# A fused fp32 transformer program on one core: stripes of eight columns in the second attention, output splits by pair, merged first tiles

## The reference, cut to what matters

```python
GRID_W, WIN_ROWS, WIN_COLS = 64, 8, 16          # 512 tokens are 8 rows of 64 columns
def neighborhood_attention(q, k, v, k_ctx, v_ctx, rpb):
    rows = n // GRID_W                           # 8
    kr = min(WIN_ROWS, rows)                     # 8: every query sees all rows
    col_start = jnp.clip(col - kc // 2, 0, GRID_W - kc)      # kc = 16
    col_mask = (col[None, :] >= col_start[:, None]) & (col[None, :] < col_start[:, None] + kc)
    def one_row(args):
        s_lat = einsum('bqhd,brkhd->bhqrk', qr, kb) * scale + bias
        s_lat = jnp.where(col_mask[...], s_lat, -jnp.inf).reshape(bsz, h, GRID_W, kr * GRID_W)
        s_ctx = einsum('bqhd,bchd->bhqc', qr, k_ctx) * scale
        p = softmax(concatenate([s_lat, s_ctx], axis=-1), axis=-1)
        o = einsum('bhqk,bkhd->bqhd', p[..., :kr * GRID_W], vb)
        return o + einsum('bhqc,bchd->bqhd', p[..., kr * GRID_W:], v_ctx)
```

## Time and profile before

| what | value |
|---|---|
| three runs, us | 2466.03, 2467.61, 2477.45; median 2467.61 |
| the profiled execution: its own time / span, us | 2472.82 / 2471.0 |
| granted TensorE clock, mean over the span | 0.989 |
| busy share | PE 96%, PE weight load 74%, DVE 48%, ACT 41%, POOL 15% |
| DMA | 77 GB/s mean, 190.64 MB |

### The profile page before, as it was taken

The page is one execution under the profiler, slowest core; times in us unless marked ns, Lnnn a source line. Parts: engine busy times, 40 slices in busy tenths (PEclk is TensorE's granted clock), DMA queues, the critical chain, the costliest instruction groups (busy, mean ns, idle before and its releaser), DMA issues.

```text
span 2471.0 us, 33313 instructions
## 1 busy us (share of the span) xinstructions
PE 2369.6 (96%) x12710; PEld 1816.9 (74%) x12710; DVE 1178.3 (48%) x1907; ACT 1010.6 (41%) x1667; POOL 376.7 (15%) x254
## 2 busy tenths in 40 slices
PE   7999999898999999989999999999999999999998
PEld 4888765466868776667776678888877667888886
DVE  5000554644442105664445556666454474666645
ACT  5111436544253425554325543333252474333422
POOL 2233001200332430003000210003400003000142
PEclk9999999999999999999999999999999999999999
DMA  7121331100231211113220122223322102322231
GB/s 309 51 69 60 116 118 48 52 1 1 65 114 60 77 60 69 53 39 105 77 85 18 35 94 94 93 94 96 100 86 86 60 1 73 98 94 94 94 101 43
DMA packets 51586, 190.64 MB, mean 77 GB/s; under 512 B 5723, under 2 KB 6107, under 8 KB 51196
## 3 DMA queue, kind: packets, MB, share of 16 engines
q1 hardware_dynamic: 51452, 188.78, 23.0%
HBM read 186.66 MB, written 2.10 MB: 76 GB/s over the span
## 4 chain that ended last, share of the span: by engine, by line
PE 89%; ACT 5%; DVE 4%; issue 2%; DMA 0%; POOL 0%; SPq 0%; DVEq 0%; ACTq 0%; POOLq 0%
PE PS L650 6%; PE PS L648 6%; PE PS L649 6%; PE PS L1772 5%; PE PS L1799 4%; PE PS L2404 3%; PE PS L2403 3%; PE PS L2405 3%; PE PS L1785 3%; PE PS L1479 3%; PE PS L602 3%; PE PS L603 3%; PE PS L601 3%; PE PS L810 2%; PE PS L808 2%; PE PS L809 2%
## 5 line engine op out<-in xcount | busy, mean ns | idle before, releaser
L648 PE MATMUL PS<-H_HI,W_SPLIT 128*128 128x512 f32 x672 | 265.5, 395 | 0.0
L650 PE MATMUL PS<-H_HI,W_SPLIT 128*128 128x512 f32 x672 | 264.9, 394 | 0.0
L649 PE MATMUL PS<-H_LO,W_SPLIT 128*128 128x512 f32 x672 | 264.5, 394 | 0.0
L497 POOL TENSOR_TENSOR W_SPLIT<-WT,W_SPLIT 128x1024 fp32r<-128x1024 f32 x43 | 104.5, 2429 | 615.9 <-ACT W_SPLIT L488 495.5
L465 ACT ACTIVATE W_SPLIT<-WT 128x1024 fp32r<-128x1024 f32 x80 | 84.8, 1060 | 267.3 <-PE PS L650 267.3
L1003 POOL TENSOR_TENSOR OUT_HALF<-WT,OUT_HALF 128x512 fp32r<-128x512 f32 x48 | 71.3, 1488 | 723.2 <-ACT OUT_HALF L967 723.2
L2758 DVE TENSOR_TENSOR W_SPLIT<-WT,W_SPLIT 128x1024 fp32r<-128x1024 f32 x80 | 98.0, 1225 | 150.1 <-ACT W_SPLIT L465 150.0
L2744 DVE TENSOR_TENSOR G_LO<-SB,G_HI 128x512 fp32r<-128x512 f32 x43 | 100.3, 2332 | 112.1 <-ACT G_HI L2565 112.1
L649 PEld LDWEIGHTS PS<-H_LO,W_SPLIT 128*128 128x128 f32 x672 | 126.0, 188 | 30.4 <-issue 0.5
L648 PEld LDWEIGHTS PS<-H_HI,W_SPLIT 128*128 128x128 f32 x672 | 126.2, 188 | 29.9 <-issue 0.5
L650 PEld LDWEIGHTS PS<-H_HI,W_SPLIT 128*128 128x128 f32 x672 | 126.2, 188 | 29.8
(11 more groups left out here) (354 smaller groups left out, 5494.6 us busy)
## 6 DMA issues: line engine op xcount, KB each, us to landing
WT<-weights SPq DMA_DIRECT2D x314, 512.0 KB, 3.5
SB<-weights SPq DMA_DIRECT2D x13, 512.0 KB, 13.4
SB<-rpb SPq DMA_DIRECT2D x8, 512.0 KB, 4.5
HT<-rpb SPq DMA_DIRECT2D x8, 512.0 KB, 4.4
XT<-tokens SPq DMA_DIRECT2D x4, 768.0 KB, 7.6
out<-HT SPq DMA_DIRECT2D x4, 512.0 KB, 3.2
SB<-late SPq DMA_DIRECT2D x1, 1280.0 KB, 5.8
SB<-con SPq DMA_DIRECT2D x1, 1248.0 KB
```

Source lines behind the costliest of these rows:

```text
L497: g.tensor_tensor(w[:, 1, :], W[:, slot, :], w[:, 0, :].bitcast(F32), ALU.subtract).then_inc(sem("w_lo"), 1)
L648: pe.matmul(PS[:, s, :], hi, H_HI[:, c, :], start=(c == 0), stop=False)
L649: pe.matmul(PS[:, s, :], hi, H_LO[:, c, :], start=False, stop=False)
L650: last = pe.matmul(PS[:, s, :], lo, H_HI[:, c, :], start=False, stop=(c == KC - 1))
```

## The change

1. **Neighbours.** att_od becomes an object of the subclass `Neighbours`. Image tokens are kept in stripes: token order is (stripe of 8 columns, row, column in the stripe), so that a stripe is 64 tokens. A step has 256 context keys and four stripes of image keys. Steps 1 to 3 take the queries of two neighbouring stripes; step 0 takes those of the two outer stripes (queries 0 to 63 and 448 to 511), whose keys are stripes 0, 1, 6, 7. The order is made where the window's norm is written (two `tensor_scalar` and two Ln with a rearranged view in place of one), and undone by the last product. Lag goes from 1 to 2, and DVE takes the first of two copy groups. The table of biases is 768 wide, not 1024.
2. **Outputs split by pair.** The splits of an output's input chunks move into the attention: ACT `split_hi` after unit u, DVE `split_lo` one step behind. PE's wait for the last product is gone; seven of tile 0's eight chunks (21 matmuls) are issued by `ahead_pe` right behind the last values and spread (in att_df ahead of the last unit's sums; in att_mla none). In att_mla the splits come in groups of 5, 2 and 1 chunks after units 3, 5 and 7.
3. **First tiles merged.** The tiles with the rotary key columns (`KROPE`) and with the gate's low rank columns (`GLR`) become one tile: 25 tiles in `ev_in`, 313 in all, every later tile one slot earlier in SP's order.
4. **The last two tiles of the last down projection** are split in the other order.

```diff
@@ Output
+            def ahead_pe(self, pe):
+                for c in range(KC - 1):
+                    self.chunk_pe(pe, 0, c)
             def pe(self, pe):
-                pe.wait_ge(sem("evac_dve"), ev_base[self.name][1])
...
@@ Output
+            def split_hi(self, act, c):
+                act.wait_ge(sem("at_out"), self.att.b["out"] + c + 1)
+                act.activation(self.O_HI[:, c, :], self.O[:, c, :], ACT.Copy).then_inc(sem("o_hi"), 1)
+            def split_lo(self, v, c):
+                v.wait_ge(sem("o_hi"), self.hi0 + c + 1)
+                v.tensor_tensor(self.O_LO[:, c, :], self.O[:, c, :], self.O_HI[:, c, :].bitcast(F32), ALU.subtract).then_inc(sem("o_lo"), 1)
@@ Pairs.act, Pairs.dve
+                    if s - self.lag - 3 in self.final:
+                        self.following.split_hi(act, self.final.index(s - self.lag - 3))
...
+                    if s - self.lag - 4 in self.final:
+                        self.following.split_lo(v, self.final.index(s - self.lag - 4))
@@ Window.split_hi
+                for k in {3: range(0, 5), 5: range(5, 7), 7: range(7, 8)}.get(u, ()):
...
+                    act.activation(self.O_HI[:, k, :], PROJ[:, ZA + self.order[k], :], ACT.Copy).then_inc(sem("o_hi"), 1)
@@ Pairs.masked
-                    if n > 512:
-                        v.tensor_tensor_reduce(out=self.SM[:, a, 512:n], in0=PS[:, self.bank(s, a) + 1, 0:n - 512],
...
+        class Neighbours(Pairs):
+            def key_parts(self, s):
+                t = self.steps[s][1]
+                if t == 0:
+                    return [(0, 0, 128), (128, 384, 512), (256, L, N)]
+                return [(0, L, N), (256, 128 * t - 128, 128 * t + 128)]
+            def queries(self, t):
+                return [(0, 0, 64), (64, L - 64, L)] if t == 0 else [(0, 128 * t - 64, 128 * t + 64)]
+            def place(self, ps, u, t):
+                return outer(ps) if t == 0 else ps[:, 128 * t - 64:128 * t + 64]
+            def last_product(self, v, dest, values, rows):
+                return v.tensor_tensor(stripes(dest), by_stripe(values), by_stripe(rows), ALU.mult)
@@ ev_in
-GLR, GK, GQ, GV, QLAT, KVLAT, KROPE, ZA, ZB = 0, 1, 3, 5, 9, 15, 17, 18, 22
-EV_CHUNKS = 26
+GLR, GK, GQ, GV, QLAT, KVLAT, ZA, ZB, ROW = 0, 1, 3, 5, 9, 15, 17, 21, 25
+EV_CHUNKS = 25
@@ feed-forward
+        def down_next(l, t):
+            return (FC - 1, FC - 2) if l == 1 and t == FC - 2 else () if l == 1 and t == FC - 1 else (t,)
```

More of the change, by code:

```diff
@@ L984, in dve @@
             def dve(self, v, add):
-                for c in range(KC):
-                    v.wait_ge(sem("o_hi"), self.hi0 + c + 1)
-                    v.tensor_tensor(self.O_LO[:, c, :], self.O[:, c, :], self.O_HI[:, c, :].bitcast(F32), ALU.subtract).then_inc(sem("o_lo"), 1)
+                self.split_lo(v, KC - 1)
                 h0 = split_at[self.following][0]
@@ L1387, in sums_ps, with split_hi, split_lo, ahead_pe @@
                 return PS[:, 6:8, :].rearrange("p b n -> p (b n)")[:, 0:N]
+            def split_hi(self, act, u):
+                for k in {3: range(0, 5), 5: range(5, 7), 7: range(7, 8)}.get(u, ()):
+                    if k >= 4:
+                        act.wait_ge(sem("at_out"), att_mla.b["out"] + 2 * (k - 4) + 2)
+                    elif k == 0:
+                        act.wait_ge(sem("at_out"), att_mla.b["out"] + 4)
+                    act.activation(self.O_HI[:, k, :], PROJ[:, ZA + self.order[k], :], ACT.Copy).then_inc(sem("o_hi"), 1)
+            def split_lo(self, v, u):
+                for k in {3: range(0, 5), 5: range(5, 7), 7: range(7, 8)}.get(u, ()):
+                    c = self.order[k]
+                    v.wait_ge(sem("o_hi"), k + 1)
+                    v.tensor_tensor(self.O_LO[:, c, :], PROJ[:, ZA + c, :], self.O_HI[:, k, :].bitcast(F32), ALU.subtract)\
+                     .then_inc(sem("o_lo"), 1)
+            def ahead_pe(self, pe):
+                pass
             def out_pe(self, pe):
@@ L1518, in out_act @@
             def out_act(self, act):
[L1519 to L1522, removed]
+                self.split_hi(act, 7)
                 for t in range(1, 8):
@@ L1600, in out_dve @@
             def out_dve(self, v):
[L1601 to L1604 removed]
+                self.split_lo(v, 7)
                 add = residual_one(v, "ev_out", N, lambda t, b: MOD[:, 16 + t, b:b + 1])
@@ L1714, in __init__ @@
                                 ("rows", 0 if gate else self.U), ("gated", self.U if gate else 0),
-                                ("half", 2 * self.S if mask and width > 512 else 0), ("out", self.U)]:
+                                ("out", self.U)]:
                     Pairs.total[name] += n
@@ L1798, in values @@
                     for a in range(2):
[L1799 to L1801 removed]
+                        x = self.PT[:, s % 2, (a * nb + c) * 128:(a * nb + c) * 128 + 128]
+                        last = pe.matmul(self.place(PS[64 * a:64 * a + 64, 6, :], u, t), self.v_of(pair, a, self.value_block(s, c)),
+                                         self.turned_block(t, x), start=(c == 0), stop=(c == nb - 1))
                 last.then_inc(sem("at_valued"), 1)
@@ L1807, in spread @@
                 for s in range(self.first[u], self.final[u] + 1):
-                    at = 128 * self.steps[s][1] - self.cols(u)[0]
+                    t = self.steps[s][1]
                     for a in range(2):
-                        last = pe.matmul(PS[64 * a:64 * a + 64, 7, at:at + 128], self.small(32, s, a).broadcast_to([128, 64]),
-                                         IDENT, start=True, stop=True)
+                        last = pe.matmul(self.place(PS[64 * a:64 * a + 64, 7, :], u, t), self.small(32, s, a).broadcast_to([128, 64]),
+                                         self.turned_block(t, IDENT), start=True, stop=True)
                 last.then_inc(sem("at_spread"), 1)
@@ L2291, in _ @@
             pe.wait_ge(sem("evac_act"), after("ev_in")[0] - 1)
-            pe.wait_ge(sem("evac_dve"), after("ev_in")[1] - 1)
+            pe.wait_ge(sem("evac_dve"), after("ev_in")[1])
             logits(0)
@@ L2373, in _ @@
             att_mla.pe(pe)
-            att_mla.wait(pe)
             pe.wait_ge(sem("gla_gated"), 1)
@@ L2380, in _ @@
             att_od.pe(pe)
-            att_od.wait(pe)
             out_od.pe(pe)
@@ L2414, in _ @@
             att_e.pe(pe)
-            att_e.wait(pe)
             out_e2.pe(pe)
@@ L2421, in _ @@
             att_df.pe(pe)
-            att_df.wait(pe)
             out_df.pe(pe)
```

201 lines of the change are left out of this document (115 added, 86 removed).

## The result

| | before | after |
|---|---|---|
| median of four runs, us | 2469.36 (2466.03 to 2477.45) | 2394.52 (2389.36 to 2395.21) |
| span of the profiled execution | 2471.0 | 2393.4 |
| PE, DVE, ACT busy, us | 2369.6, 1178.3, 1010.6 | 2309.7, 1147.9, 978.8 |
| mean granted clock | 0.989 | 0.988 |

A forecast was written before the change was run, and what follows sets the result against it. PE was taken as the bound, 89% of the chain that ended last. Terms of -59.7, -2.3, -3.9, -0.4, +1.8, -8.4, -1.9 and +0.5 sum to -74.3, from the median 2467.6 to 2393 us; range 2384 to 2406.

The forecast's parts named there:

- Second attention, -59.7: Steps go from 768 to 512 keys, 3.14 us each; a unit goes from 20.96 to 13.5 us, saving 59.7.
- Rivals A: Second attention: step 0's scores run only two tiles at a time, +6.9 us, 2400; chance 0.15.
- B: Second attention: PSUM writes in two runs cost double, about +8 to +10 us, 2402; chance 0.08.
- the bound with nothing taken off: Second attention: ACT at 12.3 and DVE at 13.3 us per unit with splits added and no work removed, under 13.5.
- Outputs: PE's waits before outputs shrink through early splits: out_od -2.3, out_e2 -2.4, ev_out -2.0 us.
- +3.2: att_mla: splits delay PE, some 2 us from the five on DVE and 1.2 from the group of two.
- att_df, +1.8: att_df and out_df: splits add 0.4 us to each of six units, +2.4; 0.7 of wait before the last sums saved.
- The part on att_e: att_e: the splits lie in idle time of both engines, so its time changes by 0.
- Clock, -3.1: Low clock behind the waits at out_e2 (-1.5 us) and ev_out (-1.6 us) goes away with them.
- ev_in -8.4: ev_in: one tile less saves 8.4 us of PE.
- last tiles -1.9: Last down projection: the whole 1.9 us wait before the last G_LAST tile goes.
- norm +0.5: Window's norm: rearranged views split one Ln in two on ACT and leave DVE's two multiplies strided, +0.5 us.

The follow-up runs named there:

- splits_only: Kernel before with only part 2, the output splits inside the attentions and 21 matmuls ahead: 2469.63 us, ratio 0.9991.
- stripes_only: Kernel before with only part 1, the second attention in stripes with its norm and bias table: 2403.65 us, ratio 0.9729.
- after_sums_first: Changed kernel with only chunk 0 of out_df's tile 0 ahead of att_df's last sums, chunks 1 to 6 behind: 2389.17 us, ratio 0.9657.
- before_mask_waits: Kernel before, but for steps of at most 512 keys DVE reduces head 0 before waiting for head 1: 2466.46 us, ratio 0.9974.
- tile_only: Kernel before with only part 3, one tile less in ev_in: 2463.69 us, ratio 0.9976.
- after_again: Changed kernel run once more, nothing edited: 2387.37 us.
- after_waits_first: Changed kernel with DVE's waits for both heads again ahead of both reductions: 2404.19 us, ratio 0.9707.
- down_only: Kernel before with only part 4, the last two tiles of the last down projection split in the other order: 2469.84 us, ratio 0.9991.
- broken_writes: Changed kernel whose second attention writes PSUM in runs of 8 or every second number, so tokens come out in another order: 2396.81 us.

## Why the prediction was right

- **Second attention, -59.7.** Right by step and size: -60.2, a unit 13.29 by 13.5. The 0.2 between is four steps of 3.11 or 3.12 rather than 3.14, and the values ahead of the spread, which follows after 0.92, not 1.03. Reading the price of a 512-key step from the causal attention, which has such steps on the same tiles, and step 0's four tiles from gated linear attention was enough. (The 20.96 counts the last spread to its end; from one unit's first scores to the next one's it is 20.89.) Rivals A (1.03 measured, 1.9 for twos) and B are out. DVE at 9.65 and ACT at 8.52 of 13.29 never came near; the bound with nothing taken off was far too high, but on the safe side.
- **Outputs.** The waits at out_od, out_e2 and ev_out went as said, -2.4, -2.2, -2.2. In att_mla the +3.2 has the right size and a wrong share: the burst of five costs 2.0 by ACT's copies and 1.06 by DVE's subtractions, 3.0 in all (splits_only), and the group of two nothing (+1.2 was charged). The +1.7 of the table is the luck of a stretch of low clock that stands on the second wait.
- **att_df, +1.8.** The table shows -0.6, because the moved wait is in it: with that alone the two stages take 124.5 (stripes_only), and with the splits on top 127.4, so the splits and their 21 matmuls cost +2.9. The step for the units was right: from sums to sums a unit takes 9.10 us in stripes_only and 9.54 in the changed kernel, +0.44 where I gave 0.4, and these six units hold 2.7 of the 2.9. The whole change shows 9.54 by 9.47, and not the 9.9 forecast, only because the moved wait took 0.37 off. The split of ACT stands right ahead of the copy for which PE's transposes wait (changed kernel; L2063 are the transposes, L990 the split, L2110 the copy):

```profile
1914.60 0.52 PE L2063 MATMUL PS<-SB 128*128 128x128 f32 x3 [0.81 <-ACT SB L2110]
```

```profile
1913.36 0.61 ACT L990 ACTIVATE O_HI<-SB 128x512 fp32r<-128x512 f32 x1
1913.88 0.57 ACT L2110 ACTIVATE SB<-PS 128x512 f32<-128x512 f32 x1
```

In stripes_only, without the split, the same wait is 0.29:

```profile
1923.39 0.52 PE L2019 MATMUL PS<-SB 128*128 128x128 f32 x3 [0.29 <-ACT SB L2064]
```

What was wrong is the small step at the end: the 0.7 of wait ahead of the last sums was to be saved. It went, but the wait behind them grew from 2.95 to 3.59, since the 21 matmuls had pushed back the start of the chain, and from the last but one sums to out_df's end the changed kernel takes 0.2 more than stripes_only. What after_sums_first gains is this wait of 3.6, which was there before too.
- **What was missed: the wait in the mask.** The part on att_e said that nothing changes there. The runs before_mask_waits and stripes_only show 1.7 to 1.9 us in att_e and 2.9 to 3.5 in att_df from a wait that the diff moves. A list of instructions alone does not show it, since they and their order are the same and only the place of a wait between them differs.
- **Clock, -3.1.** The steps "-1.5" at out_e2 and "-1.6" at ev_out count a low clock as caused by the wait ahead of it. Both stretches went, but the whole span kept 25.5 us of low clock by 25.6. And the wait alone does not bring the stretch: tile_only has the same waits (2.07 at ev_out, 2.38 at out_e2) and the full clock behind both. after_again shows that the stretches change place and number between two executions of the same program, by 10 us in sum. A term for them can't be forecast; it belongs into the range.
- **ev_in -8.4, last tiles -1.9, norm +0.5.** -8.3, -2.1, and 0 by tile_only.

That 2393 came within 2 us of 2394.5 is in part luck. The steps are mostly right, but executions of one program differ by up to 10 us, and the median before, 2467.61 when the forecast was made, is 2469.36 with a fourth run. On the traces, where 77.6 us went and not 74.3, errors partly cancel: +3.1 for the clock and +1.1 for the splits in att_df against about -5 for the moved wait, -1.5 in att_mla and -1.3 ahead of ev_in.

## What to carry to other kernels

Read in a diff not only which instructions move, but which waits change sides of an instruction: DVE that waits for both heads before the first one cost 4.6 us here. When work is moved ahead of a chain to fill a wait, look where the chain starts: fill behind its first instruction, not before it. Splits and other side work go where the gap of the engine is longer than their run: in att_mla two at a time were free where five cost 3 us, and in att_df a single one of 0.61 us cost 0.44 each time, because it stood right ahead of a copy that PE waits for. And before explaining a few us of a median, subtract the time at the lower clock stage by stage: stages then mostly agree to tenths, where executions of one program differ by up to ten. Where a stretch of low clock falls on a wait, compare with a trace that has none there: it hid 1.06 us of att_mla here.

## What was not expected of the hardware

- The granted clock falls to the lower level in stretches that cost 1.7 us or multiples, and the same program had 25.5 us of them in one execution and 15.3 in another; the thirteen traces here have from 10.2 (splits_only) to 30.7 (after_waits_first). The places are not all chance: before and down_only have the same fifteen pieces at the same places to 1 us, and broken_writes has fourteen of the changed kernel's fifteen, each 1.3 us earlier. Where none falls into a stage, PE's time for it repeats to 0.1 or 0.2 us from kernel to kernel (108.3 or 108.4 in seven of the eight traces with the striped attention).
- Matmuls that write PSUM in every second number, or in runs of 8, take the time of contiguous ones (13.29 us per unit).
- Twelve score matmuls on four 64x64 tiles (1.03 us) take no longer than four on two 64x128 tiles (1.07).

What stays open: why the stretches of low clock lie where they do, and what of the difference between 69 us (stripes_only, medians) and the 65 of its stages is more than such stretches.
